# The last layer's second feed-forward product by seven block products

## The reference

```python
def second_block(x, ...):            # after six mixer layers
    for l in range(2):
        ...                          # two kinds of attention, x = x + mixed @ w_o[l]
        h = rmsnorm(x, mlp_norm[l])
        u = square(relu(h @ w_ff1[l]))      # 1024 -> 4096
        x = x + u @ w_ff2[l]                # 4096 -> 1024
    return rmsnorm(x, final_norm)
```

## Time and profile before

| | |
|---|---|
| median of 3 runs | 2709.9 us (2709.84 to 2710.2) |
| span of the profiled execution | 2708.0 us |
| TensorE busy | 2687.0 us, 12902 matmuls |
| VectorE busy | 1551.6 us |
| ScalarE busy | 1154.0 us |
| GpSimd busy | 681.2 us |
| DMA | 238.8 MB |

### The profile page before, as it was taken

How to read it: one execution, slowest core, us unless ns; L and a number is a source line. 1 busy time by engine, 2 the same in 40 slices (tenths; PEclk the granted TensorE clock), 3 DMA queues, 4 the chain that set the end, 5 groups by cost and what they waited for, 6 DMA issues and landing times.

```text
span 2708.0 us, 32235 instructions
## 1 busy us (share of the span) xinstructions
PE 2687.0 (99%) x12902; PEld 2250.4 (83%) x12902; DVE 1551.6 (57%) x2312; ACT 1154.0 (43%) x1836; POOL 681.2 (25%) x695
## 2 busy tenths in 40 slices
PE   8999999999999999999999999999999999999999
PEld 7888888888888888888888888788888888788887
DVE  6656554344466646665575668644445558655444
ACT  4323423222347636532235767522224667522223
POOL 1000111011136626400004753411103553511100
PEclk9999999999999999999999999999999999999999
DMA  4332232323222222223322221233333211233332
GB/s 160 97 101 93 91 108 93 101 95 100 90 75 61 67 75 67 86 95 101 100 94 88 82 67 40 79 101 97 98 94 103 78 57 54 71 101 94 97 98 78
DMA packets 69414, 238.80 MB, mean 88 GB/s; under 512 B 7696, under 2 KB 10256, under 8 KB 69264
## 3 DMA queue, kind: packets, MB, share of 16 engines
q1 hardware_dynamic: 69264, 236.73, 28.1%
HBM read 234.60 MB, written 2.10 MB: 87 GB/s over the span
## 4 chain that ended last, share of the span: by engine, by line
PE 91%; DVE 4%; POOL 2%; ACT 2%; issue 0%; DMA 0%; SPq 0%; ACTq 0%; DVEq 0%
PE ps L416 29%; PE ps L418 29%; PE ps L417 29%; POOL wl L2419 2%; PE ps L552 1%; PE ps L777 1%; PE ps L776 1%; PE ps L485 0%; DVE wl L1636 0%; ACT wh L1018 0%; PE ps L613 0%; PE ps L612 0%; DVE xl L1648 0%; PE ps L470 0%; PE ps L452 0%
## 5 line engine op out<-in xcount | busy, mean ns | idle before, releaser
L1018 ACT ACTIVATE wh<-raw 128x1024 fp32r<-128x1024 f32 (+2 forms) x453 | 465.2, 1028 | 730.7 <-PE ps L418 723.7
L416 PE MATMUL ps<-xh,wh 128*128 128x512 f32 x1920 | 751.7, 391 | 0.2 <-POOL wl L2419 0.2
L418 PE MATMUL ps<-xh,wl 128*128 128x512 f32 x1920 | 747.4, 389 | 0.0
L417 PE MATMUL ps<-xl,wh 128*128 128x512 f32 x1920 | 747.2, 389 | 0.0
L1636 DVE TENSOR_TENSOR wl<-raw,wh 128x1024 fp32r<-128x1024 f32 (+1 forms) x339 | 447.7, 1321 | 156.9 <-ACT wh L1018 156.5
L416 PE MATMUL ps<-yh,wh 128*128 128x512 f32 x1088 | 425.3, 391 | 1.9 <-POOL wl L2419 1.9
L416 PEld LDWEIGHTS ps<-xh,wh 128*128 128x128 f32 x1920 | 360.5, 188 | 76.2 <-issue 1.0
L417 PE MATMUL ps<-yl,wh 128*128 128x512 f32 x1088 | 423.5, 389 | 0.0
L418 PE MATMUL ps<-yh,wl 128*128 128x512 f32 x1088 | 423.4, 389 | 0.0
L418 PEld LDWEIGHTS ps<-xh,wl 128*128 128x128 f32 x1920 | 360.4, 188 | 75.1
L417 PEld LDWEIGHTS ps<-xl,wh 128*128 128x128 f32 x1920 | 360.6, 188 | 74.8 <-issue 1.0
(11 more groups left out here) (267 smaller groups left out, 3628.6 us busy)
## 6 DMA issues: line engine op xcount, KB each, us to landing
raw<-in_ff SPq DMA_DIRECT2D x120, 512.0 KB, 3.6
raw<-in_pool_in SPq DMA_DIRECT2D x64, 512.0 KB, 3.3
raw<-in_conv_in SPq DMA_DIRECT2D x64, 512.0 KB, 3.3
raw<-in_pool_out SPq DMA_DIRECT2D x32, 512.0 KB, 3.3
raw<-in_qk SPq DMA_DIRECT2D x32, 512.0 KB, 3.7
raw<-in_pool_grp SPq DMA_DIRECT2D x16, 512.0 KB, 3.3
raw<-in_conv_out SPq DMA_DIRECT2D x16, 512.0 KB, 3.3
raw<-in_mla_z SPq DMA_DIRECT2D x16, 512.0 KB, 3.6
```

The lines of the kernel that those rows point to most:

```text
L416: pe.do.matmul(o, lh, rh_, start=start, stop=False)
L417: pe.do.matmul(o, lh, rl_, start=False, stop=False)
L418: return pe.do.matmul(o, ll, rh_, start=False, stop=stop)
L1018: act.do.activation(h[:, 0:ncol], r[:, 0:ncol], ACT.Copy).then_inc(*mark("whi", ("whi", k)))
```

## The change

In the last layer the whole second product is computed token-major. In a quarter it is the product of a matrix of 512 tokens by 1024 hidden features (two token halves by two feature halves) with one of 1024 by 1024 (two by two pieces A11, A12, A21, A22). The four blocks of the result are formed out of seven block products Q1, W5, Q6, Q2, Q7, Q3, Q4 in this order, not eight, each of 256 tokens, 512 features and 512 columns: 2 token blocks x 4 row blocks x 3 = 24 matmuls of 512 columns, on two weight units. Each has its own operands: four of them take sums of y blocks (four sums per row block, by VectorE, `t_sums`; high part by ScalarE, `t_high`; low part by VectorE, `t_low`, L1644's helper) and four take sums of weight pieces S1 to S4 (`wsum`, VectorE). The products run in three chains of banks, A, B and C: a chain's next product accumulates in the same banks, after VectorE has added the bank's present value to a block of the result or subtracted it (`post`). The weight pieces are loaded whole into memory that the attention used (`pieces`); the eight first products of a quarter come in the order 0, 4, 1, 5, 2, 6, 3, 7. The transposes of x come in quarter 0, 16 behind product 4 and 16 behind product 5, and ScalarE copies them out behind its high parts of y 5 and 6 (`turned_in`). The final norm's row work is spread over the last quarter (`row_first`, `row_second`, `row_square`, `row_scale`). The squares of the rectified products stay on GpSimd.

```diff
+FF_ORDER = (tuple(range(8)), (0, 4, 1, 5, 2, 6, 3, 7))
+PRODUCTS = ("Q1", "W5", "Q6", "Q2", "Q7", "Q3", "Q4")
+PIECES = (("A11", 0, 0), ("A21", 1, 0), ("A12", 0, 1), ("A22", 1, 1))
+WEIGHT_OF = {"Q1": "A11", "W5": "S1", "Q6": "S2", "Q2": "A12", "Q7": "S3", "Q3": "S4", "Q4": "A22"}
+CHAIN_OF = {"Q1": "A", "W5": "C", "Q6": "A", "Q2": "B", "Q7": "A", "Q3": "C", "Q4": "A"}
+CHAIN_BEFORE = {"Q6": "Q1", "Q7": "Q6", "Q4": "Q7", "Q3": "W5"}
+CHAIN_LAST = ("Q2", "Q3", "Q4")
+POST = {"Q1": (0, 0, 1), "W5": (1, 1, -1), "Q6": (0, 1, 1), "Q2": (0, 0, 1), "Q7": (1, 1, -1), "Q3": (0, 1, 1),
+        "Q4": (1, 0, -1)}
+POST_BEFORE = {"Q2": "Q1", "Q7": "W5", "Q3": "Q6"}
+ROWS_Y = {"Q1": (0, 0), "Q2": (4, 0), "Q3": (4, 256)}
+ROWS_T = {"W5": 0, "Q6": 1, "Q7": 2, "Q4": 3}
...
                 ring[0] = [home[i] for i in LAST_BANKS]
                 for qd in range(4):
...
-                        if l == 1 and qd == 3:
-                            turn_x(i // 2, i % 2)
-                    if l == 1 and qd == 3:
-                        last_product()
+                    for n in range(2 if qd == 0 else 0, 8):
+                        xgemm(st + 1, "f1", l, qd, order[n], norm=st + 1 if qd == 0 and n == 3 else None)
+                        if l == 1 and qd == 0 and n in (4, 5):
...
+                        quarter(qd)
+
+            def turn_x(half):
+                for tb in range(4):
+                    b = bank("ox", tb, half)
+                    for i in range(4):
+                        m = half * 4 + i
+                        pe.wait_ge(*at("x", 7, m))
+                        mm = pe.do.transpose(b[:, i * 128:i * 128 + 128], x[m][:, tb * 128:tb * 128 + 128], ident)
+                    mm.then_inc(*mark("group", ("mm", "ox", tb, half)))
+
+            def quarter(qd):
+                for name in PRODUCTS:
+                    ns = [unit["zq", qd, name, kk] for kk in range(2)]
+                    chain, before = CHAIN_OF[name], CHAIN_BEFORE.get(name)
+                    if before is None:
+                        for tb in range(2):
+                            bank("z" + chain, qd, tb)
+                    steps = [(kk, kp, tb) for kk in range(2) for kp in range(2) for tb in range(2)]
+                    if qd == 3 and name == "Q4":
+                        steps = [(kk, kp, tb) for tb in range(2) for kk in range(2) for kp in range(2)]
+                    for kk, kp, tb in steps:
+                        wh, wl = unit_ready(ns[kk])
+                        k = 2 * kk + kp
+                        if k == 0 and before is not None:
+                            pe.wait_ge(*at("zp", qd, before, tb))
+                        if name in ROWS_Y:
+                            y0, c0 = ROWS_Y[name]
+                            pe.wait_ge(*at("yl", "f21", qd, y0 + k))
+                            tc = slice(c0 + tb * 128, c0 + tb * 128 + 128)
+                            th, tl = YH[y0 + k][:, tc], YL[y0 + k][:, tc]
+                        else:
+                            c0 = ROWS_T[name] * 256 + tb * 128
+                            pe.wait_ge(*at("ttl", qd, k))
+                            th, tl = TT[k][:, c0:c0 + 128], TT[k][:, 1024 + c0:1024 + c0 + 128]
+                        o = ps("z" + chain, qd, tb)
+                        cc = slice(kp * S, kp * S + S)
+                        if before is None:
+                            mm = mm3(o[:, :], th, tl, wh[:, cc], wl[:, cc], k == 0, k == 3)
+                        else:
+                            mm = mm3_on(o[:, :], th, tl, wh[:, cc], wl[:, cc], k == 3)
+                        done = [("mm", "zq", qd, name, tb)] if k == 3 else []
+                        if kp == 1 and tb == 1:
+                            done.append(("wfree", ns[kk]))
+                        if done:
+                            mm.then_inc(*mark("group", *done))
 
...
+                def ff_high(qd, i):
+                    if qd:
+                        act.wait_ge(*at("mm", "zq", qd - 1, "Q4", 1))
+                    cc = slice(0, 256) if i < 4 else slice(0, 512)
+                    high(YH[i][:, cc], temp("ff", l, qd, i)[:, cc], ("ffs", l, qd, i), ("yh", "f21", qd, i))
+
+                def turned_in(half):
+                    act.wait_ge(*at("mm", "ox", 3, half))
+                    for i in range(4):
+                        act.wait_ge(*at("xl", 7, 4 * half + i))
+                    for tb in range(4):
+                        act.do.activation(zblock(half, tb), ps("ox", tb, half)[:, :], ACT.Copy).then_inc(
+                            *mark("act", ("xt", half, tb), ("psfree", "ox", tb, half)))
+
+                def t_high(qd, k):
+                    high(TT[k][:, 0:1024], TS[:, :], ("tsum", qd, k), ("tth", qd, k))
...
+                        weights(unit["f1", l, qd, i] + AHEAD[min(n, 4) if qd == 0 else 4])
...
+                        if n and n % 2 == 0:
+                            t_high(qd, n // 2 - 1)
+                        ff_high(qd, i)
+                        if qd == 0 and n in (5, 6):
+                            turned_in(n - 5)
...
+                    else:
+                        t_high(qd, 3)
+                        for name in PRODUCTS:
+                            for kk in range(2):
+                                taking("zq", qd, name, kk)
+                                if qd == 3:
+                                    last_rows(name, kk)
...
+            def row_square(half, tb, col):
+                act.wait_ge(*at("z", half, tb))
+                act.do.activation(XH[4 * half + tb][:, :], zblock(half, tb), ACT.Square, accum_out=sc(col, tb)).then_inc(
+                    *mark("act", ("zs", half, tb)))
+
+            def row_scale(half, tb):
+                act.wait_ge(*at("zsum", tb))
+                act.wait_ge(*at("zs", half, tb))
+                act.do.activation(sc(20, tb), sc(20, tb), ACT.Sqrt, bias=sc(24, tb), scale=1.0 / 1024).then_inc(
+                    *mark("act", ("zroot", tb)))
+                act.wait_ge(*at("zrec", tb))
+                o = zblock(1 - half, tb)
+                act.do.activation(o, o, ACT.Copy, scale=sc(28, tb)).then_inc(*mark("act", ("o", tb, 1 - half)))
+
+            def last_rows(name, kk):
+                if name == "Q7":
+                    row_square(0, kk, 16)
+                elif name == "Q3":
+                    row_square(1, 2 + kk, 16)
+                elif name == "Q4":
+                    row_square(0, 2 + kk, 20)
+                    row_scale(0, 2 + kk)
...
+            for tb in range(2):
+                row_square(1, tb, 20)
+                row_scale(1, tb)
...
+                def t_sums(qd, k):
+                    y, y4 = temp("ff", l, qd, k), temp("ff", l, qd, k + 4)
+                    t1, t2, t3, t4 = [TS[:, 256 * n:256 * n + 256] for n in range(4)]
+                    dve.wait_ge(*at("ffs", l, qd, k + 4))
+                    dve.do.tensor_tensor(t1, y[:, 0:256], y[:, 256:512], ALU.subtract).then_inc(
+                        *mark("dve", ("t1n", qd, k)))
+                    dve.do.tensor_tensor(t3, y4[:, 256:512], y[:, 256:512], ALU.subtract)
+                    dve.wait_ge(*at("t1n", qd, k))
+                    dve.do.scalar_tensor_tensor(t2, t1, -1.0, y4[:, 256:512], ALU.mult, ALU.subtract).then_inc(
+                        *mark("dve", ("t2n", qd, k)))
+                    dve.wait_ge(*at("t2n", qd, k))
+                    dve.do.scalar_tensor_tensor(t4, t2, -1.0, y4[:, 0:256], ALU.mult, ALU.subtract).then_inc(
+                        *mark("dve", ("tsum", qd, k), ("tfree", "ff", l, qd, k), ("tfree", "ff", l, qd, k + 4)))
...
+                def t_low(qd, k):
+                    low(TT[k][:, 1024:2048], TS[:, :], TT[k][:, 0:1024], ("tth", qd, k), ("ttl", qd, k))
...
+                def wsum(qd, name, kk, a, b):
+                    cc = slice(kk * 1024, kk * 1024 + 1024)
+                    dve.wait_ge(*at("wsrc", qd, a, kk))
+                    dve.wait_ge(*at("wsrc", qd, b, kk))
+                    dve.do.tensor_tensor(RB[name][:, cc], RB[a][:, cc], RB[b][:, cc], ALU.add).then_inc(
+                        *mark("dve", ("wsrc", qd, name, kk)))
...
+                def post(qd, name, tb):
+                    half, tok, sign = POST[name]
+                    z = zblock(half, 2 * tok + tb)
+                    dve.wait_ge(*at("mm", "zq", qd, name, tb))
...
+                    p = ps("z" + CHAIN_OF[name], qd, tb)[:, :]
+                    done = [("zp", qd, name, tb)]
...
+                    if sign > 0:
+                        dve.do.tensor_tensor(z, p, z, ALU.add).then_inc(*mark("dve", *done))
+                    else:
+                        dve.do.tensor_tensor(z, z, p, ALU.subtract).then_inc(*mark("dve", *done))
+
+                def quarter(qd):
+                    for n, name in enumerate(PRODUCTS):
+                        for kk in range(2):
+                            taking("zq", qd, name, kk)
+                            if n:
```

(83 more changed lines are left out.)

186 lines of the change are left out of this document (82 added, 104 removed).

## The result

| | before | after |
|---|---|---|
| median, four runs each | 2709.9 us | 2736.7 us (2735.6 to 2737.9) |
| ratio, 95% interval | | 1.0099 (1.0084 to 1.0113) |
| span of the profiled execution | 2708.0 us | 2736.1 us |
| matmuls | 12902 | 12806 |
| last quarter's last matmul to last scaled row | 3.2 us | 7.8 us |

What follows compares the result with a forecast made beforehand. TensorE, busy 2687.0 of 2708.0 us, was taken as the bound. Terms -21.8 + 16.0 + 2.0 + 13.6 + 1.2 + 5.2 + 0.8 = +17.0 gave a 2725.0 us span and 2727 us median, range 2713 to 2738.

Steps and rivals of the forecast that it cites:

- Matmuls, -21.8: Last layer's second product: 672 matmuls instead of 768, 96 fewer at 0.227 us, 21.8 us less TensorE work.
- Quarter 0, +16.0: First product of quarter 0: second run of transposes waits for banks behind VectorE's chain, delaying product 6; +16.0 us net.
- Clock once, +2.0: Behind some 9 us of unbroken TensorE idle time in quarter 0, nine matmuls run at the slow clock: +2.0 us.
- Starts of the second products, +13.6: Each quarter, TensorE waits for VectorE at W5's second unit and Q6's second block: 3.4 us, +13.6 for four.
- Q4's second unit, +1.2: Last quarter: ScalarE's row squares stand ahead of high parts, so Q4's second unit is ready late: +1.2 us.
- Tail, +5.2: After the last matmul: chained row blocks on VectorE and ScalarE take 8.0 us against 2.8: +5.2.
- Restarts and later begin, +0.8: TensorE's first matmul after a wait lasts 0.47 instead of 0.39 us; ten restarts, +0.8 us.
- DMA, 0: Weight loads: same volume, 32 blocks of 512 KB, costed at nothing, with 2 us of cover in quarter 0.
- the first (banks): Rival, faster: ring of banks decides; with early copies of transposes the stall is 6 instead of 16 us; chance 0.09.
- The third: Rival: VectorE bounds the first product too, 42 of 43.5 us; each quarter costs 5.5; 2735, up to 2742; chance 0.14.
- The fourth: Rival: accumulating on in a bank VectorE just read costs 0.1 us at 32 places, +3, inside the range.
- The no-difference rival: Second rival: terms at their low ends and the tail hidden as well, 2710 to 2715 us; chance 0.07.

Runs made afterwards that it cites:

- the run with filled waits: Changed kernel plus 16 unread matmuls per quarter in TensorE's wait before W5's second unit: 2734.1 us.
- dealing the blocks out: Changed kernel with the last four row blocks' finish interleaved on VectorE and ScalarE: 2732.7 us.
- other banks: Changed kernel with another order of banks for the transposes and ScalarE copying them out earlier: 2727.2 us.
- the last version above: Scheme in quarters 1 to 3, squares on ScalarE, start reordered, tail interleaved, half of S2 behind product 5, ScalarE's row squares later: 2695.6 us.
- the first order: Changed kernel with the first half of weight sum S2 moved behind the low part of W5's second unit: 2735.5 us.
- the second order: Changed kernel, W5's second unit's low part before the last token sums' low part, Q1's additions before Q6's second unit's low part: 2728.1 us.
- the four-quarter kernel: Changed kernel, scheme in all quarters, with squares on ScalarE, the second order, interleaved tail and other banks: 2704.8 us.

## Why the prediction was right, and where it was too low

The profiled spans differ by 28.1 us, where +17.0 were forecast for them.

- **Matmuls, -21.8:** right. 96 fewer, the new form at 0.227 us.
- **Quarter 0, +16.0:** right in mechanism and size. Product 6 starts at 2403.99 instead of 2382.7; less 0.5 by which this part begins later and less the 3.9 of the old transposes, this is +16.9. TensorE waits 8.26 us where 9 were named, and the copy that releases it is the one named.
- **Clock once, +2.0:** right behind that wait: 12 matmuls took 5.14 instead of 2.72 us, +2.4. The count of nine was short: at the start of the program 12 matmuls, from 6.46 to 13.22 us, last 0.63 us or more, the length at this pace.
- **Starts of the second products, +13.6:** the step that failed, in size. The four second products measure 43.3, 44.6, 44.9 and 44.7 us, ideal is 38.08; less Q4's share this is +24.0. The mechanism (VectorE's chain ending at W5's second unit) was right, with two terms wrong. The wait is 3.67 us and not 2.1. In quarter 1 VectorE comes to product 7 at 1.75 us and not at 1.1, since squares make low parts 0.28 us longer on average and single steps 0.84 longer. And from the low part before it to the last low part of y there was one square of 0.7 us in my chain; the trace has 1.67, since VectorE stands idle while GpSimd squares and ScalarE makes the high part. Second, I charged the clock once, for the 9 us wait, and never asked whether 3 us would do the same. It did, four times. By the run with filled waits, VectorE's lateness makes 20.5 of the 24.0 us and the slow clock, net, 3.6. The 1.1 us at Q6's second block was right only where the clock stayed up: in the kernel after the slow matmuls hide it; with the wait filled it appears as 0.71.
- **Q4's second unit, +1.2:** 1.1 (0.94 of wait and the restart).
- **Tail, +5.2:** +4.6, from 3.2 to 7.8 us; dealing the blocks out gave 3.0 of it back, 2 of them in the span.
- **Restarts and later begin, +0.8:** 0.5 us of later begin are of this size, but they are not this kernel's: its trace has the clock down near 1627 and 2245 us as well (0.91 in 1620 to 1640, 1.00 in the kernel before), in stretches that the change doesn't touch, and other kernels here begin the part up to 0.2 us earlier or 1.5 later. The restarts lie inside the measured products.
- **DMA, 0:** right. Neither TensorE nor ScalarE, which takes the weights' loads, waits for one between 2352 and 2725 us.

The measured terms, -21.8 + 16.9 + 2.4 + 24.0 + 1.1 + 4.6 + 0.5, make +27.7 of 28.1.

The **rivals:** the first (banks) would have been faster; with other banks VectorE's waits took their place, so the ring alone doesn't decide the sign. The third is wrong in its reason (VectorE is busy for 34 of 43 us in a first product and not 42, less even than the 38 of my own sum, and first products run at 43.5 us without loss), but its price for the start of a second product, 5.5 us, was nearer than my 3.4: the measured ones, less Q4's share, are 5.2, 6.5, 6.8 and 5.5. The fourth, a price for going on in a bank just read, is out: in the last version above the three second products take 38.1 us each, 168 matmuls at 0.227. The no-difference rival was wrong.

## What to carry to other kernels

This scheme, which trades matmuls for additions, paid only once the engine that adds was ahead at the moment when TensorE asked. So write down that engine's chain at each start of a product, with what it waits for, and not its average load. Where a wait of a few us is forecast, price the lower clock behind it too, and then see who is late next, since part of it may come back. GpSimd's work beside a VectorE on the critical chain was the first thing to move here.

## What the runs showed of the hardware

Waits of 2.1 to 3.7 us lowered TensorE's granted clock to 0.50 in the middle of a full kernel: in all four second products of the kernel after (3.26 to 3.67 us) and of the first order (2.12 to 2.53), though not after the same 3.67 us in one quarter of the kernel with other banks; after two of four waits of 2.4 with the second order; and not after 2.2 and 2.3 us in quarter 0 of the four-quarter kernel. No wait of 1.3 us at a second product's start lowered it. The Trainium skill (TensorE: Matmul & The Clock Gate, "Part 1: The HAM clock gate") has the throttled state as the default that activity lifts; the fall and the recovery agree, but what tells the two outcomes of the same wait apart stays open. It may also be what spreads the times, 2735.6 to 2737.9 here against 2709.7 to 2710.2 before; no run separates this.
